# Splitting the DMA issues of an attention stage over three queues: pages for VectorE on SyncE, strips' pages and residual halves on ScalarE, transposes' inputs on GpSimd

## What is computed

```python
hp, (k1, v1, lf1, _) = even_mixer(hp, *ew, past=None)                # the prompt, causal over its 2048 positions
hs, (k2, v2, lf2, vb2) = even_mixer(hs, *ew, past=(cache_k[j], cache_v[j], cache_logf[j], page_table))
```

## Time and profile before

| what | value |
|---|---|
| median of three executions | 3896.78 us |
| the profiled execution | 3896.33 us |
| its span, first to last instruction | 3894.6 us |
| what lies around the span | 1.7 us |
| mean granted TensorE clock | 0.922 |
| busy over the span: TensorE, VectorE, ScalarE, GpSimd | 86%, 52%, 21%, 4% |
| attention stage, on the trace's time axis | 1057 to about 2193 us |

### The profile page before, as it was taken

How to read it: one execution, slowest core, us unless ns; L and a number is a source line. 1 busy time by engine, 2 the same in 40 slices (tenths; PEclk the granted TensorE clock), 3 DMA queues, 4 the chain that set the end, 5 groups by cost and what they waited for, 6 DMA issues and landing times. The chain is left out here.

```text
span 3894.6 us, 43985 instructions
## 1 busy us (share of the span) xinstructions
PE 3334.3 (86%) x14087; PEld 1778.0 (46%) x14087; DVE 2012.4 (52%) x3042; ACT 810.8 (21%) x1512; POOL 162.2 (4%) x294
## 2 busy tenths in 40 slices
PE   2999999997278887888888689999999999847799
PEld 1444444443133333333332267676776767612343
DVE  1778888886445565676575114444344443413211
ACT  1111111111032231232223022223222232102111
POOL 0000000000110000000000000000000000000000
PEclk8999999998679888999899889999999999976899
DMA  5566666666044645544455330000000000154331
GB/s 210 174 192 196 195 195 197 203 199 201 24 149 141 206 125 159 170 149 148 141 163 154 101 136 22 11 11 22 11 22 11 11 22 11 22 75 129 109 113 71
DMA packets 231782, 447.99 MB, mean 115 GB/s; under 512 B 38529, under 2 KB 61057, under 8 KB 230586
## 3 DMA queue, kind: packets, MB, share of 16 engines
q1 hardware_dynamic: 205130, 391.14, 32.8%
q0 software_dynamic: 11904, 39.85, 2.9%
q10 hardware_dynamic: 14592, 15.24, 1.2%
HBM read 390.16 MB, written 55.99 MB: 115 GB/s over the span
## 5 line engine op out<-in xcount | busy, mean ns | idle before, releaser
L523 PE MATMUL ep_PJ<-ep_w,ep_xT 128*128 128x512 f32 x1792 | 782.4, 595 | 10.4 <-ACT ep_xT L383 10.4
L523 PEld LDWEIGHTS ep_PJ<-ep_w,ep_xT 128*128 128x128 f32 x1792 | 337.8, 191 | 420.6 <-issue 414.2
L1800 PE MATMUL mb_B<-ml_w,mp_xT 128*128 128x512 f32 x1024 | 446.4, 594 | 0.0
L444 DVE TENSOR_TENSOR ep_kpage<-ep_kpage,ep_q_bc 128x1024 f32<-128x1024 f32 x256 | 311.2, 1216 | 129.0 <-DMA ep_kpage<-in_cache_k_dram 128.8
L452 DVE TENSOR_REDUCE g_scores<-ep_kpage 128x1024 f32 (+1 forms) x256 | 311.2, 1216 | 11.5 <-DVE ep_kpage L444 3.3
L1076 DVE TENSOR_REDUCE at_mpart<-at_S 128x2 f32<-128x1024 f32 (+3 forms) x160 | 170.1, 1063 | 283.4 <-PE at_S L1225 169.4
L1036 ACT ACTIVATE at_PT<-at_S,g_negc 128x512 f32<-128x512 f32 (+3 forms) x320 | 181.8, 619 | 643.8 <-PE at_S L1253 527.4
L1800 PEld LDWEIGHTS mb_B<-ml_w,mp_xT 128*128 128x128 f32 x1024 | 192.0, 190 | 230.1 <-issue 229.6
L1813 PE MATMUL mb_B<-mp_xT,ml_w 128*128 128x128 f32 x2048 | 253.0, 290 | 0.0
L1813 PEld LDWEIGHTS mb_B<-mp_xT,ml_w 128*128 128x128 f32 x2048 | 250.5, 206 | 0.0
L2318 PE MATMUL fi_O<-ml_w,fi_yT 128*128 128x512 f32 (+1 forms) x544 | 236.6, 593 | 0.0
(11 more groups left out here) (460 smaller groups left out, 3700.6 us busy)
## 6 DMA issues: line engine op xcount, KB each, us to landing
ep_kpage<-in_cache_k_dram SPq DMA_DIRECT2D x512, 256.0 KB, 2.9
at_vpage<-in_cache_v_dram SPq DMA_DIRECT2D x256, 256.0 KB, 2.9
at_spage<-in_cache_v_dram SPq DMA_DIRECT2D x256, 256.0 KB, 3.0
ep_w<-in_even_w_in_dram SPq DMA_DIRECT2D x8, 1796.0 KB, 30.2
ml_w<-in_odd_w_in_dram SPq DMA_DIRECT2D x24, 512.0 KB
ep_x<-in_x_prompt_dram SPq DMA_DIRECT2D x16, 512.0 KB
scratch_mix<-ep_mixed SPq DMA_DIRECT2D x16, 512.0 KB, 3.0
at_xh<-in_x_prompt_dram POOLq DMA_DIRECT2D x32, 256.0 KB, 3.8
```

The source lines that it names most:

```text
L444: nc.vector.tensor_tensor(kpage[i][:], kpage[i][:], q_bc[r][:].unsqueeze(1).to_broadcast([P, 2, AW]), ALU.mult).then_inc(pr[i], 1)
L523: op = nc.tensor.matmul(BANK[name][:], xT[r][:, k, :], w[:, k, COL[name]:COL[name] + 512], start=k == 0, stop=k == KC - 1)
L1800: op = nc.tensor.matmul(B[banks[m]][:], xT[:, k, :], w[:, k, col + 512 * m:col + 512 * m + 512], start=k == 0, stop=k == KC - 1)
```

## The change

`loads_at` goes away. SyncE issues VectorE's pairs only. The loads of the strips (`strip_pair`) and of the residual halves (`residual_in`, `residual_out`) move, with their waits, into ScalarE's stream. There `transfers(i)` stands between `exp(i)` and the evacuations of step i and issues the strips' loads and the writes of step i - 1 and the residual reads of step i - 2. In the tail the writes and reads of step i follow `transfers(i)` directly. GpSimd keeps the inputs of the turns and the values, and may issue an input one step earlier (`i + 3` for `i + 2`).

```diff
--- before.py
+++ after.py
@@ -833,11 +833,6 @@
         def in_step(ends, i):
             return range(ends[i - 1] if i else 0, ends[i])
 
-        loads_at = [[] for _ in range(STEPS + TAIL)]
-        for i in range(STEPS + TAIL):
-            loads_at[i] += [("v", d + 2) for d in in_step(d_end, i) if d + 2 < PAIRS]
-            loads_at[i] += [("s", 2 * g + r) for g in in_step(s_end, i) for r in (3, 4) if 2 * g + r < 2 * GROUPS]
-
         late = [[] for _ in range(STEPS + TAIL + 1)]
         for i in range(STEPS + TAIL):
             here = []
@@ -899,22 +894,12 @@
                 for j in range(2):
                     page(4 * d + j, vpage[d % 2][:, j, :], vp_in[d % 2])
 
-            def strip_pair(n):
-                if n >= 3:
-                    sp.wait_ge(paged, 4 * ((n - 3) // 2 + 1))
-                for j in range(2):
-                    page(4 * n + 2 + j, spage[n % 3][:, j, :], sp_in[n % 3])
-
             for n in range(2):
                 weighed_pair(n)
-            for n in range(3):
-                strip_pair(n)
             for i in range(STEPS + TAIL):
-                for kind, n in loads_at[i]:
-                    if kind == "v":
-                        weighed_pair(n)
-                    else:
-                        strip_pair(n)
+                for n in in_step(d_end, i):
+                    if n + 2 < PAIRS:
+                        weighed_pair(n + 2)
 
         @block.gpsimd
         def _(pool):
@@ -966,34 +951,17 @@
             def values_in(g):
                 pool.dma_start(V[:, 4 * g:4 * g + 4, :], io["v_prompt"][512 * g:512 * g + 512, :].rearrange("(t p) c -> p t c", p=P)).then_inc(v_in[g], 16)
 
-            def residual_in(y):
-                if y >= 2:
-                    pool.wait_ge(x_put[y % 2], 16 * (y // 2))
-                pool.dma_start(xh[y % 2][:], io["x_prompt"][(y // 2) * P:(y // 2 + 1) * P, 512 * (y % 2):512 * (y % 2) + 512]).then_inc(x_got[y % 2], 16)
-
-            def residual_out(y):
-                pool.wait_ge(h_ready, y + 1)
-                pool.dma_start(io["h1"][(y // 2) * P:(y // 2 + 1) * P, 512 * (y % 2):512 * (y % 2) + 512], xh[y % 2][:]).then_inc(x_put[y % 2], 16)
-
             got = 0
             while got < len(loads) and loads[got] < t_end[0]:
                 stage_in(got)
                 got += 1
             values_in(0)
-            residual_in(0)
-            residual_in(1)
             for i in range(STEPS + TAIL):
-                while got < len(loads) and loads[got] < t_end[min(i + 2, STEPS + TAIL)]:
+                while got < len(loads) and loads[got] < t_end[min(i + 3, STEPS + TAIL)]:
                     stage_in(got)
                     got += 1
                 if i % 8 == 0 and 1 <= i // 8 < GR:
                     values_in(i // 8)
-                for y in y_at[i]:
-                    residual_out(y)
-                    if y + 2 < 2 * NT:
-                        residual_in(y + 2)
-            for r in range(2):
-                pool.wait_ge(x_put[r], 16 * NT)
 
         @block.scalar
         def _(act):
@@ -1035,11 +1003,45 @@
                     h = 2 * (u % HP) + hh
                     nc.scalar.activation(PT[i % 2][:, hh, 0:n], S2[:, hh, 0:n], ACT.Exp, bias=keep["negc"][:, j, h:h + 1]).then_inc(exped, 1)
 
+            def strip_pair(n):
+                if n >= 3:
+                    act.wait_ge(paged, 4 * ((n - 3) // 2 + 1))
+                for j in range(2):
+                    k = 4 * n + 2 + j
+                    at = act.value_load(pages[k // PAGES:k // PAGES + 1, k % PAGES:k % PAGES + 1], min_val=0, max_val=N_PHYS - 1)
+                    act.dma_start(spage[n % 3][:, j, :], io["cache_v"][bass.ds(at * P, P), :]).then_inc(sp_in[n % 3], 16)
+
+            def residual_in(y):
+                if y >= 2:
+                    act.wait_ge(x_put[y % 2], 16 * (y // 2))
+                act.dma_start(xh[y % 2][:], io["x_prompt"][(y // 2) * P:(y // 2 + 1) * P, 512 * (y % 2):512 * (y % 2) + 512]).then_inc(x_got[y % 2], 16)
+
+            def residual_out(y):
+                act.wait_ge(h_ready, y + 1)
+                act.dma_start(io["h1"][(y // 2) * P:(y // 2 + 1) * P, 512 * (y % 2):512 * (y % 2) + 512], xh[y % 2][:]).then_inc(x_put[y % 2], 16)
+
+            def transfers(i):
+                for g in in_step(s_end, i - 1) if i else ():
+                    for n in (2 * g + 3, 2 * g + 4):
+                        if n < 2 * GROUPS:
+                            strip_pair(n)
+                for y in y_at[i - 1] if 0 < i <= STEPS else ():
+                    residual_out(y)
+                for y in y_at[i - 2] if 1 < i < STEPS + 2 else ():
+                    if y + 2 < 2 * NT:
+                        residual_in(y + 2)
+
+            act.wait_ge(pages_in, 16)
+            for n in range(3):
+                strip_pair(n)
+            residual_in(0)
+            residual_in(1)
             for e in range(t_end[0]):
                 evacuate(e)
             held = []
             for i in range(STEPS):
                 exp(i)
+                transfers(i)
                 for e in held:
                     evacuate(e)
                 held = late[i] if turns[t_end[i + 1] - 1][0] == "z" else []
@@ -1048,8 +1050,18 @@
                         evacuate(e)
             for e in held:
                 evacuate(e)
-            for e in range(t_end[STEPS], TE):
+            for i in range(STEPS, STEPS + TAIL):
+                for e in range(t_end[i], t_end[i + 1]):
+                    evacuate(e)
+                transfers(i)
+                for y in y_at[i]:
+                    residual_out(y)
+                    if y + 2 < 2 * NT:
+                        residual_in(y + 2)
+            for e in range(t_end[STEPS + TAIL], TE):
                 evacuate(e)
+            for r in range(2):
+                act.wait_ge(x_put[r], 16 * NT)
 
         @block.vector
         def _(dve):
```

## The result

The changed kernel takes 3927.36 us, the median of five executions (3925.18 to 3937.51). Before takes 3894.11 us beside it. The ratio is 1.0091, with a 95% interval of 1.0071 to 1.0112, so the change costs about 0.9%. The forecast of no change was wrong, though its range of 3852 to 3932 holds the time. The profiled execution has a span of 3925.6 us against 3894.6.

What follows compares the result with a forecast made beforehand. TensorE was taken to set the pace, busy 929 of 1145 us in the stage. Gains of 45 + 31 = 76 us against costs of 54 + 20 = 74 gave 2 us less, 3895 us, range 3852 to 3932.

Steps and rivals of the forecast that it cites:

- forecast of no change: Whole kernel: gains and costs cancel within 20 us, 3875 to 3915, likeliest 3895 us; chance 0.48.
- gain 1: Inputs of the turns on GpSimd no longer wait behind residuals: 31 us of TensorE's waits and 14 of clock, 45 us.
- gain 2: Strips' pages no longer wait behind VectorE's on SyncE: 25 us of TensorE's waits and 6 of clock, 31 us.
- cost 1: ScalarE's queue: 4.4 us per group of four pages delays exponentials and evacuations, 42 us and 12 of clock, 54 us.
- cost 2: Tail: strips' pages issued behind the residual's write and read, 17 us of stalls and 3 of clock, 20 us.
- tail's three waits: Strips' pairs 123, 125 and 127 in the tail: TensorE stalls 8.8, 1.8 and 8.8 us.
- 25 places: Steps with a strips' group: later work on ScalarE delayed, each place losing 0.5 to 4.3 us, in sum 53.
- the clock's part of the sum: TensorE's half clock around waits: 14 and 6 us in the gains, 12 and 3 in the costs.
- ScalarE becomes the pacer: Rival: block between exponential and evacuation, 4.4 us or more per group, outlasts its room; 37 us slower, 3933; chance 0.20.
- waits for `h_ready` on top: ScalarE's block between exponential and evacuation: these waits add to its 4.4 us or more per group; no separate size.
- ScalarE hardly feels it: Rival: page numbers are fetched during exponentials, slack takes the rest; ScalarE's queue costs 12, total 3853 us; chance 0.27.
- The pages are late of themselves: Rival: two queues stretch landings on shared DMA engines, strips' waits stay; 29 us slower, 3925; chance 0.05.

Runs made afterwards that it cites:

- e2: Changed kernel with the strips' loads back on SyncE; residuals stay on ScalarE, inputs alone on GpSimd: 3863.36 us, ratio 0.9934.
- e7: Changed kernel with strips' pages issued from GpSimd ahead of the inputs, which may go one more step ahead: 3831.34 us, ratio 0.9846.
- e1: Changed kernel with the strips' loads ahead of the residual's write and read in the tail: 3903.11 us, ratio 1.0033.
- e9: Kernel of e2 with inputs only as far ahead as before (`i + 2` for `i + 3`): 3865.28 us, ratio 0.9926.
- e4: Changed kernel with strips' pages read at fixed places, without the look-up of page numbers: 3877.53 us, ratio 0.9968.
- e3: Changed kernel with residuals and inputs back on GpSimd as before, strips' pages still on ScalarE: 3927.13 us, ratio 1.0098.
- e6: Kernel of e2 with VectorE's pair that must wait for a finished sequence's turn later in SyncE's list: 3843.76 us, ratio 0.9879.
- e3_again: Same kernel as e3, run again for another profile: 3918.78 us, ratio 1.0085; median of all ten executions 3922.8 us.

## Why the forecast was wrong

By its own steps, in us. "Profile" is from the stretches above, "medians" from the runs' medians, with before at 3891.2 us as in those groups and not at the 3894.1 of the first comparison.

| step | forecast | profile | medians |
|---|---|---|---|
| gain 1, inputs freed (e2 against before) | 45 | 35 | 28 |
| gain 2, strips freed (e7 against e2) | 31 | 21 | 32 |
| cost 1, ScalarE's block (after against e7; medians: e1 against e7) | 54 | 60 | 72 |
| cost 2, the tail (after against before; medians: against e1) | 20 | 26 | 24 |
| sum | -2 | +30 | +36 |

The two columns on the right differ by what single executions scatter. Both tell the same in the main: every mechanism of the forecast is there, gain 1 was sized too large and both costs too small. Gain 2 came as forecast by the medians, but measured on GpSimd, where the pages may also go out earlier than on ScalarE. What that is worth stands under cost 1 here.

**What was right.** The strips and inputs stood behind foreign waits, and freeing them removes those waits (e2, e7, e9). A page costs ScalarE 1.08 us. The tail's three waits sum to 22.1 us where 19.4 were counted. The forecast laid out 53 us of lost time behind ScalarE in 25 places, and TensorE's four waits for ScalarE are 54 us longer in the changed kernel (83.7) than in e7_pool (30.1). VectorE's pages gate TensorE at a finished sequence, so only about half of the strips' wait is gained. VectorE's wait for the inverted sums went from 37.4 to 59.5 us, against 70 forecast.

**Which step failed.** It is the clock's part of the sum: 14 and 6 us in the gains, 12 and 3 in the costs. By these terms TensorE would get 5 us back. Taking its idle and busy time apart shows what came:

| part | forecast | measured in the profiles |
|---|---|---|
| gain 1: idle, clock | 31, 14 | 26.5, 8.1 |
| gain 2: idle, clock | 25, 6 | 25.1, -3.9 |
| cost 1: idle, clock | 42, 12 | 40.4, 19.3 |
| cost 2: idle, clock | 17, 3 | 19.8, 5.8 |

The idle time was forecast to grow by 3 us and grew by 8.6. The busy time was to shrink by 5 us through the clock and grew by 20.9. So 26 of the 31 us that the profiled execution is off lie in the clock, and the total is well beyond the 7 us by which one profile's busy time scatters. A single row is not: with e9_ahead's profile in place of e2's, the clock's part of gain 1 is 15 and not 8. By the medians most of the error stands in gain 1 (17 us too much) and in cost 1 (18 too little).

TensorE's work is the same in all kernels. Counting each busy microsecond at half clock as half, the steps hold 782 to 783 us in the profiles of before, after, e2 and e7, worked out by laying the record of the granted clock over TensorE's busy time. The time at half clock is also the same before and after: 181 and 182 us. But before, 127 us of it were work and 54 idle time. After, 155 us were work and 27 idle. The same record, laid over TensorE's idle stretches, shows which ones had held the slow clock. Before, three stretches of over 7.5 us held 26 of the 54 us. After, none is as long. Those of 2 to 5 us add up to 66 us in both kernels, with 5 and 9 us at half clock in them. My reading is that the few longest waits had soaked up slow clock, and that with them gone it fell on matmuls. No run varied the length of waits alone, so this is argued from the sums. I had priced the clock from two stretches, at 14 us for 31 of waits in gain 1 and 12 us for 42 in cost 1, as if it went with the waits added and taken away.

**The rivals.** "ScalarE becomes the pacer" came closest in what happened: 3933 forecast, 3927 measured. It was to cost by the length of the block, and so it does: e4 shows that with a short one the change gains. At which length it turns was not tried. Its further ground, waits for `h_ready` on top, finds little support. Moving residuals and inputs is worth 28 us where ScalarE issues no page (e2) and still 20 us where it does (3922.8 of e3's kernel against 3903.1 of e1), so by these medians those waits cost some 8 us there at most. "ScalarE hardly feels it" fell with e4 and e7. "The pages are late of themselves" is closest by the number, 3925, and that is luck: it has gain 2 at nothing, and gain 2 measures 21 to 32 us. A strip's page does land later in the changed kernel, and that lengthened the tail's first wait. Strips' pages before, then after:

```profile
DMA to landing us min/median/max: 2.4/3.0/5.8
```

```profile
DMA to landing us min/median/max: 2.4/3.4/7.1
```

Yet the waits for pages fall as soon as the order lets them (e6: 29.1, e7: 17.3). The rule of the Trainium skill that I named against the change (DMA: Bandwidth & Descriptors, Issuing engines are not separate DMA queues) speaks of the 16 shared engines, and there the trace agrees: the DMA share of the steps is 0.50 before and after. Its conclusion that only the time to initiate is saved does not hold here. Each queue issues in order, as the earlier trace rows show, and a transfer behind a foreign wait is late whatever the engines do. Taking transfers out from behind such waits was worth 28 us for the inputs and 20 to 32 for the strips.

## What to carry to other kernels

Look on each DMA queue for loads that stand behind a wait which isn't theirs: reordering the list (e6) or an idle engine's queue (e7) frees them. Don't put a block of register work and issues on an engine whose results others wait for. Here four pages at 1.08 us each between an exponential and its evacuations cost more than all that the change freed. If such a block must be there, it belongs behind the evacuations (30 us here). When transfers move to another stream, check its last steps by themselves, where one wait stands ahead of everything. And don't count on all the clock coming back with a wait that goes: here the time at half clock was the same before and after, and more of it fell on work.

## What the runs showed that was not expected

Look-ups of page numbers start on ScalarE's queue while the exponential is still at work, so the block begins early (the first issue at 1124.01, the exponential's end at 1124.36), and yet its whole rest is idle time of the engine (3.25 us). An issue takes 0.35 us on ScalarE's queue and 0.54 on GpSimd's, and GpSimd's strips land in 3.7 us in the median, but e7, with the slowest issues, is the fastest kernel: what matters is who waits behind them. Ten executions of one kernel (e3_strips, e3_again) spread from 3905 to 3933 us. Its two profiles differ in the clock alone, for which I have no cause.
